# w_in's first units by halves of the channels, new ring slots, and new tiles at the two seams of a two-block transformer kernel

## The reference

```python
a = rms_norm(h, attn_norm);  proj = a @ w_in            # first stage, T_IN
h = h + concat(y_mla, y_swa) @ w_out
m = rms_norm(h, mlp_norm)
h = h + square(relu(m @ w_up)) @ w_down                 # MLP1
x = rms_norm(h, final_norm)                             # seam "f"
z = modulated(x) @ w_in_2 ...                           # stage T_Z
x = layer_norm(ALPHA*x + gate*(...@ w_o + b_o))         # seam "ln1"
x = x + gate*(square(relu(modulated(x) @ w_m1)) @ w_m2) # MLP2
```

## Time and profile before

| | us |
|---|---|
| median of 3 runs | 2429.3 (2428.83 to 2429.86) |
| the execution that was profiled | 2428.58 |
| its span, first to last instruction | 2426.8 |
| PE busy in the span | 2376.5 (98%) |
| DVE busy | 1710.0 (70%) |
| ACT busy | 1049.4 (43%) |
| DMA | 230 GB/s in the mean |

### The profile page before, as it was taken

The page is one execution under the profiler, slowest core; times in us unless marked ns, Lnnn a source line. Parts: engine busy times, 40 slices in busy tenths (PEclk is TensorE's granted clock), DMA queues, the critical chain, the costliest instruction groups (busy, mean ns, idle before and its releaser), DMA issues.

```text
span 2426.8 us, 30941 instructions
## 1 busy us (share of the span) xinstructions
PE 2376.5 (98%) x13376; PEld 2051.0 (85%) x13376; DVE 1710.0 (70%) x1559; ACT 1049.4 (43%) x999; POOL 29.8 (1%) x61
## 2 busy tenths in 40 slices
PE   7999999999999999989999999999999999999998
PEld 7998888888778888878888888997888888888887
DVE  7777577878777777765677666787764566774665
ACT  5464544434334334455645443343543443443443
POOL 0000000000000000000000000000000000000000
PEclk9999999999999999999999999999999999999999
DMA  7334477777777787775545547875455557775553
GB/s 274 134 130 151 174 262 287 288 290 271 280 294 278 296 309 285 299 268 189 211 162 181 184 177 269 299 278 200 173 190 197 186 190 301 273 278 211 186 193 110
DMA packets 79816, 558.73 MB, mean 230 GB/s; under 512 B 9034, under 2 KB 11285, under 8 KB 13248
## 3 DMA queue, kind: packets, MB, share of 16 engines
q1 hardware_dynamic: 74832, 528.25, 58.9%
q0 software_dynamic: 4848, 28.50, 3.3%
HBM read 547.26 MB, written 9.45 MB: 229 GB/s over the span
## 4 chain that ended last, share of the span: by engine, by line
PE 90%; DVE 4%; DMA 3%; ACT 2%; issue 1%; SPq 0%; ACTq 0%; DVEq 0%
PE ps L582 27%; PE ps L585 13%; PE ps L613 12%; PE ps L615 12%; PE ps L614 12%; DMA stage<-wstream 3%; PE ps L550 2%; PE ps L551 2%; PE ps L552 2%; DVE w_lo L1509 2%; ACT w_hi L1055 1%; PE ps L580 1%; PE ps L625 1%; PE ps L627 1%; PE ps L626 1%
## 5 line engine op out<-in xcount | busy, mean ns | idle before, releaser
L1509 DVE TENSOR_TENSOR w_lo<-stage,w_hi 128x2048 fp32r<-128x2048 f32 x402 | 918.4, 2288 | 459.0 <-ACT w_hi L1055 455.1
L1055 ACT ACTIVATE w_hi<-stage 128x2048 fp32r<-128x2048 f32 x402 | 766.6, 1911 | 755.1 <-DMA stage<-wstream 402.8
L582 PE MATMUL ps<-xs,w_hi 128*128 128x512 f32 x3200 | 998.5, 397 | 16.1 <-DVE w_lo L1509 14.0
L585 PEld LDWEIGHTS ps<-xs,w_lo 128*128 128x128 f32 x3000 | 564.9, 188 | 132.0
L585 PE MATMUL ps<-xs,w_lo 128*128 128x256 f32 x3000 | 591.6, 279 | 0.0
L582 PEld LDWEIGHTS ps<-xs,w_hi 128*128 128x128 f32 x3200 | 495.7, 189 | 31.2 <-DVE w_lo L1509 17.6
L613 PE MATMUL ps<-w_hi,hs 128*128 128x512 f32 x1008 | 394.4, 391 | 0.0
L615 PE MATMUL ps<-w_lo,hs 128*128 128x512 f32 x1008 | 392.7, 390 | 0.0
L614 PE MATMUL ps<-w_hi,hs 128*128 128x512 f32 x1008 | 392.6, 389 | 0.0
L613 PEld LDWEIGHTS ps<-w_hi,hs 128*128 128x128 f32 x1008 | 189.3, 188 | 41.7 <-issue 2.2
L614 PEld LDWEIGHTS ps<-w_hi,hs 128*128 128x128 f32 x1008 | 189.3, 188 | 39.7 <-issue 0.7
(11 more groups left out here) (414 smaller groups left out, 2248.2 us busy)
## 6 DMA issues: line engine op xcount, KB each, us to landing
stage<-wstream SPq DMA_DIRECT2D x497, 1024.0 KB, 4.9
spectra<-k_made POOLq DMA_DIRECT2D x4, 1024.0 KB, 7.7
k_spec<-spectra POOLq DMA_DIRECT2D x4, 1024.0 KB, 6.4
xraw<-xT SPq DMA_DIRECT2D x4, 512.0 KB, 11.4
resid<-x SPq DMA_DIRECT2D x2, 1024.0 KB, 15.7
w<-w POOLq DMA_DIRECT2D x16, 128.0 KB, 5.9
parked<-resid POOLq DMA_DIRECT2D x1, 2048.0 KB, 7.4
resid<-parked POOLq DMA_DIRECT2D x1, 2048.0 KB, 9.0
```

The costliest lines, as they stand in the source:

```text
L582: mm = pe.matmul(out[c], hi[c], rhs[:, k, :], start=(first and j == 0), stop=end)
L585: mm = pe.matmul(out[c][:, S:2 * S], lo[c], rhs[:, k, 0:S], start=False, stop=False)
L1055: act.activation(w_hi[:, w % HIGH, 0:m], stage[:, n % RING, 0:m], ACT.Copy).then_inc(hi_ready, 1)
L1509: tt(w_lo[:, slot, 0:m], stage[:, slot, 0:m], f(w_hi[:, w % HIGH, 0:m]), ALU.subtract).then_inc(lo_ready, 1)
```

## The change

Five things at once:

1. **Slots.** `slots()` gives each position of the stream the slot that should come free first (a w tile at its number plus 1, an a tile at the number of the w tile before it less 1.1), in place of `n % RING`. `HELD_BY[n]` is the position whose use the load of n waits for. It differs from n-5 at most positions from 48 on.
2. **Start.** Tiles 0 to 3 of w_in in the order k0 = 0 of units 0 and 1, then k0 = 8 of both. Tile 0 is loaded and split in two halves (chunks 0 to 3, chunks 4 to 7), the second load behind x group 0. POOL's six loads wait for x group 2. DVE makes split(2) ahead of `positions()`, and `chunk_steps(0)` and (1) move one step later; ACT loads the table of the square root ahead of the squares; both make split(4) after the token root.
3. **Splits at the seams.** Steps 169 and 273 are no longer left out: tiles 171 and 275 are split there.
4. **Turns at the seams.** Only blocks 0 and 1 are turned ahead of the first tile; block 2 in the middle of the first, block 3 in the middle of the second. Block 0 is turned chunks 0 and 1 first (`first_turned`). ACT makes the high part of chunks 0 and 1 before its own chunks 2 and 3 (`first_hi`). Banks are 4, 6, 4, 6 (before: 4, 6, 2, 4).
5. **Tiles at the seams.** The first two tiles hold four chunks for two units each (`quad`, `by_quarters`): tile T_Z chunks 0 to 3, tile T_Z+1 chunks 4 to 7; the next two have k0 = 8 of one unit each, as before. The same at T_MLP2.

```diff
-CHUNK = {1: 0, 2: 1, 4: 2, 5: 3, 6: 4, 7: 5}
+CHUNK = {2: 0, 3: 1, 4: 2, 5: 3, 6: 4, 7: 5}
+def slots():
+    free, uses = [-1.0 + i / RING for i in range(RING)], [0] * RING
+    held, k = [None] * RING, 0
+    slot, use, held_by = [], [], []
+    for n, (kind, i) in enumerate(ORDER):
+        k = i if kind == "w" else k
+        s = min(range(RING), key=lambda j: free[j])
+        uses[s] += 1
...
+        held[s] = n
+        free[s] = k + 1.0 if kind == "w" else k - 1.1
+    return slot, use, held_by
...
+    if w in (T_Z, T_Z + 1):
+        return "quad", U_Z, 4 * (w - T_Z)
+    if w in (T_MLP2, T_MLP2 + 1):
+        return "quad", U_MLP2, 4 * (w - T_MLP2)
...
-    TURN = (4, 6, 2, 4)
+    TURN = (4, 6, 4, 6)
...
         for n in range(RING, len(ORDER)):
-            kind, k = ORDER[n - RING]
+            kind, k = ORDER[HELD_BY[n]]
...
+        sp.dma_start(stage[:, 0, 0:half], ws[0][:, 0:half]).then_inc(sem("first_loaded"), 16)
         sp.dma_start(cols[:], dram["cols"]).then_inc(sem("cols_loaded"), 16)
         for g in range(4):
...
-            if g % 2:
-                load(1 + g // 2)
+            if g == 0:
+                sp.dma_start(stage[:, 0, half:], ws[0][:, half:]).then_inc(loaded[0], 16)
+            if g == 1:
+                load(1)
+        load(2)
         load(3)
...
+        pool.wait_ge(sem("x_loaded_2"), 16)
         pool.dma_start(pos_i[:], dram["pos_q"]).then_inc(sem("pos_loaded"), 16)
...
+        def two_units(w, rhs, k0, u, first, ready, hook):
+            for j in range(4):
+                k = k0 + j
+                if j == 2:
+                    hook()
+                if j % 2 == 0:
+                    pe.wait_ge(*ready(k // 2))
+                for v in range(2):
...
+            if n >= 2:
+                pe.wait_ge(sem("seam_lo"), since(name, "lo") + n)
...
-        for n in range(3):
+        for n in range(2):
             turn_normed("f", n)
...
-                 (lambda: turn_normed("f", 3)) if w == T_Z else None)
+                 (lambda: turn_normed("f", 2 + w - T_Z)) if w < T_Z + 2 else None)
...
-        def into_stage(name, sh, sc, w):
+        def into_stage(name, sh, sc):
             act.wait_ge(sem("seam_scaled"), since(name, "scaled") + 1)
             scale_block(name, 2)
-            normed_hi(name, 0, sh, sc, w)
+            first_hi(name, sh, sc)
+            normed_hi(name, 1, sh, sc)
             scale_block(name, 3)
-            for n in range(1, 4):
-                normed_hi(name, n, sh, sc, w)
+            for n in range(2, 4):
+                normed_hi(name, n, sh, sc)
...
         for w in range(T_IN, T_QB):
...
+            if w == 2:
+                dve.wait_ge(sem("consts_loaded"), 48)
+                chunk_steps(1)
+                take_bias(0)
+            elif w != 3:
+                split(w + 2)
             if w == 0:
-                chunk_steps(0)
-            split(w + 2)
+                positions()
...
         for w in range(T_MLP1, T_Z):
-            if w not in LAST:
-                split(w + 2)
-                condition(w + 2)
+            split(w + 2)
+            condition(w + 2)
...
             normed_lower(name, 2, sh, sc)
-            split(w)
             normed_lo(name, 2)
```

More of the change, by code:

```diff
@@ L108 @@
 WHERE = {what: n for n, what in enumerate(ORDER)}
+def slots():
[6 more added lines that the diff above has]
+        uses[s] += 1
+        slot.append(s)
+        use.append(uses[s])
+        held_by.append(held[s])
+        held[s] = n
+        free[s] = k + 1.0 if kind == "w" else k - 1.1
+    return slot, use, held_by
+SLOT, USE, HELD_BY = slots()
 def place(w):
@@ L576, in both_halves @@
                 hi = [w_hi[:, w % HIGH, (j * 2 + c) * P:(j * 2 + c) * P + P] for c in range(2)]
-                lo = [w_lo[:, place(w) % RING, (j * 2 + c) * P:(j * 2 + c) * P + P] for c in range(2)]
+                lo = [w_lo[:, SLOT[place(w)], (j * 2 + c) * P:(j * 2 + c) * P + P] for c in range(2)]
                 if end:
@@ L586, in both_halves @@
             return mm
+        def two_units(w, rhs, k0, u, first, ready, hook):
[6 more added lines that the diff above has]
+                for v in range(2):
+                    out = [ps[:, 2 * ((u + v) % 2) + c, :] for c in range(2)]
+                    a = [1024 * v + (j * 2 + c) * P for c in range(2)]
+                    for c in range(2):
+                        pe.matmul(out[c], w_hi[:, w % HIGH, a[c]:a[c] + P], rhs[:, k, :], start=(first and j == 0),
+                                  stop=False)
+                    for c in range(2):
+                        mm = pe.matmul(out[c][:, S:2 * S], w_lo[:, SLOT[place(w)], a[c]:a[c] + P], rhs[:, k, 0:S],
+                                       start=False, stop=False)
+            return mm
         def tokens_apart(w, rhs, k0, u):
@@ L915, in mlp @@
                 if l < UPT:
-                    if t0 == T_MLP2 and w == t0 + 1:
-                        pe.wait_ge(sem("seam_lower"), since("ln1", "lower") + 3)
-                        pe.wait_ge(sem("seam_upper"), since("ln1", "upper") + 3)
-                    tile(w, xs, rhs_ready if w < t0 + 4 else None, hook if w == t0 else None)
+                    turn = (lambda: hook(2 + w - t0)) if hook is not None and w < t0 + 2 else None
+                    tile(w, xs, rhs_ready if w < t0 + 4 else None, turn)
                     if after is not None and w == t0:
@@ L939, in turn_normed @@
                 pe.wait_ge(sem("seam_scaled"), since(name, "scaled") + n)
[L940 to L942 removed]
+            if n >= 2:
+                pe.wait_ge(sem("seam_lo"), since(name, "lo") + n)
+            if n == 0:
+                for half in range(2):
+                    for t in range(NB):
+                        pe.wait_ge(sem("seam_normed"), since(name, "normed") + t + 1)
+                        for c in range(2):
+                            a = P * (2 * half + c)
+                            mm = pe.transpose(ps[:, TURN[0] + half, c * S + t * P:c * S + t * P + P],
+                                              resid[:, t, a:a + P], ident[:])
+                    mm.then_inc(sem("seam_turned" if half else "first_turned"), 1)
+                return
+            turn_block(n, TURN[n]).then_inc(sem("seam_turned"), 1)
         def turn_input(i):
@@ L1079, in token_root, with first_hi, normed_hi @@
             act.activation(root_[:], var[:], ACT.Sqrt).then_inc(sem("token_root_ready"), 1)
-        def normed_hi(name, n, sh, sc, w):
+        def first_hi(name, sh, sc):
+            act.wait_ge(sem("seam_lower"), since(name, "lower") + 1)
+            act.activation(xs[:, 0:2, 0:S], turned[:, 0, 0:2], ACT.Copy).then_inc(sem("seam_hi"), 1)
+            act.wait_ge(sem("seam_turned"), since(name, "turned") + 1)
+            src = turned_bank(TURN[0])
+            for k in (2, 3):
+                ins = act.activation(turned[:, 0, k], src[:, k, :], ACT.Identity, bias=mod[:, sh + k:sh + k + 1],
+                                     scale=mod[:, sc + k:sc + k + 1])
+            ins.then_inc(sem("seam_upper"), 1)
+            act.wait_ge(sem("seam_upper"), since(name, "upper") + 1)
+            act.activation(xs[:, 2:4, 0:S], turned[:, 0, 2:4], ACT.Copy).then_inc(sem("seam_hi"), 1)
+        def normed_hi(name, n, sh, sc):
             act.wait_ge(sem("seam_turned"), since(name, "turned") + n + 1)
@@ L1132, in _ @@
                     sem("xin_hi"), 1)
+            if g == 0:
+                act.wait_ge(loaded[0], 16)
+                act.activation(w_hi[:, 0, half:], stage[:, 0, half:], ACT.Copy).then_inc(hi_ready, 1)
             if g == 1:
@@ L1546, in took_done @@
             dve.nop().then_inc(evac_done, 1)
-        split(0)
+        half = TILE // 2
+        dve.wait_ge(sem("first_hi"), 1)
+        tt(w_lo[:, 0, 0:half], stage[:, 0, 0:half], f(w_hi[:, 0, 0:half]), ALU.subtract).then_inc(sem("first_split"), 1)
         dve.wait_ge(sem("cols_loaded"), 16)
@@ L1558, in _ @@
                 ins.then_inc(sem("xin_ready"), 1)
+            if i == 3:
+                dve.wait_ge(hi_ready, 1)
+                tt(w_lo[:, 0, half:], stage[:, 0, half:], f(w_hi[:, 0, half:]), ALU.subtract).then_inc(lo_ready, 1)
             if i == 7:
@@ L1680, in _ @@
             _, u, _ = job(w)
-            if ends(w) and w > 1:
+            if ends(w) and w > 2:
                 summed(dve, u, w)
@@ L1930, in normed_lower @@
         def normed_lower(name, n, sh, sc):
-            dve.wait_ge(sem("seam_turned"), since(name, "turned") + n + 1)
+            if n:
+                dve.wait_ge(sem("seam_turned"), since(name, "turned") + n + 1)
+            else:
+                dve.wait_ge(sem("first_turned"), ("f", "ln1").index(name) + 1)
             src = turned_bank(TURN[n])
```

111 lines of the change are left out of this document (55 added, 56 removed).

## The result

The changed kernel is slower: 2459.7 us (2456.7 to 2460.3, four runs) against 2429.4 us (2428.8 to 2429.9, four runs), a ratio of 1.012 (1.0105 to 1.014). The prediction was 2420.1, between 2408 and 2427.

The account below looks back on a forecast made before the run. PE was taken as the bound, so only its waits and clock could give time. 2428.6 - 12.7 (MLP1) - 3.4 (start) + 2.4 (seam "f") + 4.5 (seam "ln1") = 2419.4, or 2420.1 against the median 2429.3; range 2408 to 2427.

Parts of the forecast that it names:

- What bounds the kernel: Whole kernel: PE is 90% of the chain; only its waits, some 45 of 2427 us, and its clock can give time.
- Slots (MLP1): MLP1: w tile loads issued 4.6 to 5.6 us earlier, all eight PE waits gone: -12.7 us, bounds -13.0 and -6.
- the clock's 1.7: MLP1: 3.4 us of PE work at clock 0.50 after the wait of 2.49 us loses 1.7 us, to be regained.
- The other stages with a tiles: Stages with a tiles outside MLP1: no such waits there, so nothing counted.
- Start: Start: first matmul near 9.8, DVE's run and tile 4 (39.5 to 40.2) earlier: -3.4 us, bounds -1.5 and -4.1.
- Seam "f": Seam "f": three short waits become one of 3.7 us before tile 172, clock 0.50 after: +2.4 us, bounds -3.3 and +3.5.
- rival A: Both seams: third tile not held, waits inside go, -3.3 at "f", -1.5 at "ln1"; 2408.4 us, sign waits below 1 us; chance 0.20.
- Seam "ln1": Seam "ln1": as at "f", plus second token half 1.2 us later behind split(275): +4.5 us, bounds -1.5 and +6.
- C: MLP1: SP keeps order, loads wait for nearer a tiles, 0.1 us for each of 70: 2439.8 us; chance with D 0.06.
- D: MLP1: no effect, as POOL's 1 MB writes slow the loads: near 2432.8 us; chance with C 0.06.
- B: MLP1: slots give only half, -6.3 us, as loads behind a tiles wait for DVE: 2426.5 us; chance 0.14.

Follow-up runs that it names:

- the holder mended: The kernel before with the new slots alone, an a tile's slot reckoned free at k - 0.5 instead of k - 1.1: 2413.9 us, ratio 0.9935.
- the other number: Slots constant 0.5 in place of 1.1: on the changed kernel 2416.0 us; on the kernel before with the new slots alone 2413.9 us.
- the kernel with the third split early: Changed kernel with slots constant 0.5, the third tile split before block 3 at both seams: 2405.0 us, ratio 0.9902; again 2405.8 us.
- the last two experiments: Against the kernel with the third split early: split(275) moved into seam "ln1", 2404.4 us; POOL's wait for x removed, 2407.8 us.

## Why the prediction was wrong, by its own steps

**What bounds the kernel.** Right for the kernel before: PE, and only its waits could give time. What the views did not tell, and I did not ask, is how near the next bound lay. SP's loads waited 1.2 us for DVE's products in the kernel before; a ring that hands the slot of a product to the next w tile puts product and split on the path of every load.

**Slots (MLP1), the step that failed.** "Tile k waits for tile k-4, or for the a tile two positions ahead, which DVE is done with some 6.5 us after PE begins two tiles before that: about 1 us after PE ends k-4." I had read `HELD_BY` rightly, and even the two positions. The time of the product I took from PE's pace (PE begins a tile, ACT 1.9, DVE 2.3 and 2.3), as if its load were always there. But that load is itself one of those that wait for a product, and the product stands in DVE's program behind the split of the w tile before it, which waits for its own load. For a 44 the rule gives 804.3 + 6.5 = 810.8 (PE began tile 124 when it ended 123, at 804.32); it was done at 815.23, 4.4 us later, because tile 126, ahead of it, was itself issued only at 803.91 behind the product of a 43. "So the load is issued 4.6 us earlier at the least", before PE ends tile k-3, came true for one of the 54 w tiles of MLP1 that wait for an a tile: they were issued between 5.0 us before and 3.6 us after that end, 0.1 us after it in the median, no earlier than with the old slots. An open sum of delays can't show that; adding up one round can: two loads of 4.9, ACT's 1.9, DVE's 2.3 and two products of 2.2 are 18.4 us for three w tiles, against 16.8 of PE at the prediction's own 5.6 us each, all from durations that stood in the earlier trace rows. The short round is 4.9 + 1.9 + 2.3 + 2.2 = 11.3 us for two w tiles, against 11.2. `HELD_BY` has 16 rounds of the long kind and 37 of the short in MLP1, and 16 times 1.6 with 37 times 0.1 is an estimate of 29 us by which the loads fall behind PE: sign and order of size were to be had without a run (PE's waits came to 24.1 us).

How much was then to be had: -15.1 us with the holder mended, more than the -12.7 forecast and than the bound of -13.0. The bound was made of the waits and the clock alone. With the slots mended the trace of MLP1 has no waits and no stretch at 0.50, and held against it tile by tile the kernel before loses 11.3 us in its eight waits, 2.1 us on top of them (0.25 to 0.28 us in each such tile: tile 109 took 7.53 us with a wait of 1.69, and 5.58 without) and 1.5 us by the clock. The term that was missing is the 2.1; the clock's 1.7 was 0.2 too much.

**The other stages with a tiles**, counted at nothing: +2.0 us behind tile 242. There too loads wait for an a tile two positions ahead and are issued 0.04 us after its product, and PE waits for other work that DVE comes to late (1.06 us for `mixacc`, 0.41 for `tev`). With the slots alone it was +3.8 us, with the other number it is gone, so there the loop is the cause. For the changed kernel that is shown only in part: with its new slots undone the stage still took 1.3 us more (two waits for `tev`), and why stays open.

**Start.** Right: -3.4 forecast, -4.0 measured in this trace; -2.7 to -4.1 in the other seven with the same start, and 4.2 by the times of two kernels that differ in it alone. The first matmul came at 10.27 (forecast 9.8); tile 4 began at 39.59 (forecast 39.5 to 40.2), and the wait for r_x before it stayed:
```profile
10.27 0.55 PE L580 MATMUL ps<-xin,w_hi 128*128 128x256 f32 x1 [10.27 <-DVE xin L1629]
...
38.20 1.56 PE L843 MATMUL ps<-rel_part,steps 128*128 128x64 bf16 x48 [0.89 <-DVEq L1756]
39.59 0.36 PE L580 MATMUL ps<-xin,w_hi 128*128 128x256 f32 x1
```
The mechanism is the one forecast, the shift of DVE's run and not the earlier start of PE. But two terms were off and partly cancelled: tile 2 landed at 18.95 (forecast 19.5 to 20.35), so the run began at 20.93 (21.5 to 22.3), and from there to tile 4 passed 18.7 us (17.95). Nor did POOL's bytes leave tile 2's load alone, as the forecast had it: without POOL's wait it landed at 20.78.

**Seam "f".** Right in mechanism and size: +2.4 forecast, +2.6 measured. The wait of 3.7 us before the third tile was 3.58, and the clock behind it 0.50 for 3.4 us of work. Waits below 1 us, the sign of rival A, came only when the split or the turn was moved, in another kernel than this one. The Trainium skill's page "TensorE: Matmul & The Clock Gate", Part 1, states that the throttled clock is the default and that activity releases it; that one long wait then costs more than three short ones is my reading of it. Here the trace agrees: behind the three short waits of the kernel before (0.29, 0.87 and 1.35 us) the clock stayed at 1.00, and behind the 3.58 us it fell to 0.50, at both seams.

**Seam "ln1".** Right in mechanism, a little too high: +4.5 forecast, +3.6 measured. The 1.2 us of the second token half were 1.25 (5.79 less the 4.54 in the trace of the kernel before, 4.6 in the earlier trace rows), and the third tile waited 3.58 us as at "f". DVE has the split of tile 275 ahead of the first token half, as forecast (timeline of DVE, kernel after):
```profile
1713.72 2.29 DVE L1581 TENSOR_TENSOR w_lo<-stage,w_hi 128x2048 fp32r<-128x2048 f32 x1 [1.94 <-ACT w_hi L1116]
1715.93 0.68 DVE L2223 TENSOR_TENSOR step_t<-ps,g_row 128x512 f32<-128x512 f32 x1
```
The 0.9 us between lie in the stretch from the first transpose to the third tile: 20.85 us (1743.68 less 1722.83), forecast 21.9; "f" had 20.8, forecast 20.8. My addition of 1.1 us for the longer low clock at "ln1" was the part too much: the clock was indeed low for 4.6 us behind the first transpose there, and for 3.4 us at "f", and the two stretches took the same time.

**The rivals.** It was C, with its mechanism named (SP keeps to its order, a load waits for the a tile two or three ahead) and its chance, with D, at 0.06. What I wrote against it, "DVE's extra work for the filters is 2.3 us in a step", asks whether some extra work makes DVE late; no extra work was needed, for the chain was late by its own length. Its price, 0.1 us for each of 70 a tiles, had no row behind it: it was 23.9 + 12.7 us above the forecast for MLP1 and not 7 + 12.7, because the cost falls on the sixteen long rounds, some 2 us each, and five of the sixteen waits cost clock as well. B and D fell: the slots gave not half but less than nothing, and with the other number all eight waits went, with POOL's writes as before. A did not come: the third tile was held at both seams.

## What to carry to other kernels

Where buffers of a ring go to the user that is "free first", write down who frees each one and follow it round: if the load of a tile waits for work that its engine does behind a tile loaded just before, the ring is a closed loop, and its round must be added up (load, each step, in program order) and held against the time of the bounding engine for as many tiles. Here moving one constant of the slots from 1.1 to 0.5 opened the ring and turned +1.0% into -0.65%. The queue that issues the loads shows such a loop at once in the table of waits: what it waits for changes from the bounding engine to the one that frees the slots. And a step moved to remove small waits should be followed to what it now stands behind: one split placed in an idle gap of 4 us made the two new seams 4 to 5 us better than the old ones in place of 6 us worse.

## What the runs showed of the hardware

A wait doesn't fix what the clock does next. Waits of 2.53 and 2.32 us in MLP1 were followed by 0.50 for 3.4 us, one of 2.48 us, at 865.70, was not, though the kernel before had paid after 2.49; one of 1.76 us, at 895.94, was, with another wait of 2.48 us 28 us ahead of it. After the 4.03 us at 775.14 the clock stayed low for 6.8 us, twice the usual. Nor does the length of the wait fix how long the clock stays low: the same wait of 3.77 us before the first transpose of seam "f" was followed by 3.4 us at 0.50 in seven traces and by 6.8 us in six, and the kernel with the third split early had one of each in two executions. In a loop that makes PE wait again and again this came to 8.8 us on top of 24.1 us of waiting, where the kernel before had 1.5 on top of 11.3.

A wait costs PE more than the idle time that the table gives: 0.25 to 0.32 us more in every tile of MLP1 that had one, in both kernels.

Time from the first instruction to the first matmul varied between 10.01 and 11.17 us in eight traces with the same start; that alone is a microsecond of scatter, as much as the last two experiments were to tell apart.
